# A ring of two buffers in place of three for the split blocks of w_in in the prompt phase

## What is computed

```python
h = rms_norm(x, norm1)
p = h @ w_in                      # 1024 -> 3080 columns: u, v of the gMLP; q, k, v, z; beta, a
y_a = rms_norm(u * (W_s @ gelu(v) + b_s))                # group A, in blocks of 128 rows
q, k, v = silu(causal_conv(q, k, v))                     # group B: width 4, then the gated delta rule
o, S = gated_delta_chunked(q, k, v, g, beta, S0, chunk)  # state S is carried from tile to tile
x = x + concat(y_a, rms_norm(o) * silu(z)) @ w_o
x = x + (silu(h2 @ w_gate) * (h2 @ w_up)) @ w_down       # h2 = rms_norm(x), d_ff = 2816
```

## Time and profile before

| | us |
|---|---|
| median of three executions | 3152.46 |
| lowest and highest | 3148.61, 3154.37 |
| the profiled execution | 3150.51 |
| its span in the trace | 3148.8 |

### The profile page before, as it was taken

How to read it: one execution, slowest core, us unless ns; L and a number is a source line. 1 busy time by engine, 2 the same in 40 slices (tenths; PEclk the granted TensorE clock), 3 DMA queues, 4 the chain that set the end, 5 groups by cost and what they waited for, 6 DMA issues and landing times.

```text
span 3148.8 us, 42004 instructions
## 1 busy us (share of the span) xinstructions
PE 2943.8 (93%) x17132; PEld 2690.0 (85%) x17132; DVE 1418.4 (45%) x2017; ACT 984.2 (31%) x1620; POOL 164.5 (5%) x156
## 2 busy tenths in 40 slices
PE   7689998999998987789999999999999999999998
PEld 6478787878887876689999999999999999999998
DVE  3355556555555543435333343553333335434344
ACT  3233544444444434323212211332112124222212
POOL 2000111111111111200000000000000000000000
PEclk9689999999999988899999999999999999999999
DMA  5245333433333333042122221521222215222220
GB/s 204 76 134 171 98 112 105 130 103 108 96 92 90 115 124 60 15 131 80 54 67 62 65 59 53 187 68 53 67 67 67 62 44 174 81 80 74 73 80 34
DMA packets 352683, 284.44 MB, mean 90 GB/s; under 512 B 14141, under 2 KB 322434, under 8 KB 350514
## 3 DMA queue, kind: packets, MB, share of 16 engines
q1 hardware_dynamic: 352562, 282.78, 29.6%
HBM read 236.97 MB, written 45.78 MB: 90 GB/s over the span
## 4 chain that ended last, share of the span: by engine, by line
PE 54%; DVE 1%; ACT 1%; issue 1%; DVEq 0%; POOL 0%; ACTq 0%; POOLq 0%
PE gate_ps L2828 7%; PE gate_ps L2829 6%; PE gate_ps L2830 6%; PE up_ps L2828 6%; PE up_ps L2829 6%; PE up_ps L2830 6%; PE down_ps L2828 5%; PE down_ps L2829 5%; PE down_ps L2830 5%; DVE w_in_sb L2767 0%; ACT h_hi L2661 0%; DVE w_in_sb L2761 0%; DVE w_in_sb L2822 0%; ACT w_hi L2607 0%; ACT h_hi L2626 0%
## 5 line engine op out<-in xcount | busy, mean ns | idle before, releaser
L2134 PE MATMUL pr_p<-hT_hi_p,w_hi_p 128*128 128x512 f32 x800 | 344.0, 430 | 24.0 <-ACT w_in_sb L1670 21.3
L2828 PE MATMUL gate_ps<-h_hi,w_hi 128*128 128x384 f32 (+1 forms) x1056 | 345.6, 327 | 3.6 <-DVE h_lo L2773 3.4
L2830 PE MATMUL gate_ps<-h_hi,w_lo 128*128 128x384 f32 (+1 forms) x1056 | 345.3, 327 | 0.0
L2829 PE MATMUL gate_ps<-h_lo,w_hi 128*128 128x384 f32 (+1 forms) x1056 | 345.1, 327 | 0.0
L2828 PE MATMUL up_ps<-h_hi,w_hi 128*128 128x384 f32 (+1 forms) x1056 | 344.2, 326 | 0.0
L2829 PE MATMUL up_ps<-h_lo,w_hi 128*128 128x384 f32 (+1 forms) x1056 | 343.9, 326 | 0.0
L2830 PE MATMUL up_ps<-h_hi,w_lo 128*128 128x384 f32 (+1 forms) x1056 | 343.9, 326 | 0.0
L2711 DVE TENSOR_TENSOR w_in_sb<-up_ps,w_in_sb 128x384 f32<-128x384 f32 (+1 forms) x132 | 70.7, 536 | 597.8 <-PE up_ps L2830 597.8
L2136 PE MATMUL pr_p<-hT_hi_p,w_lo_p 128*128 128x512 f32 x800 | 318.6, 398 | 0.0
L2135 PE MATMUL pr_p<-hT_lo_p,w_hi_p 128*128 128x512 f32 x800 | 317.3, 397 | 0.0
L2723 DVE TENSOR_TENSOR w_in_sb<-down_ps,w_in_sb 128x1024 f32<-128x1024 f32 x187 | 228.7, 1223 | 182.8 <-PE down_ps L2830 182.8
(11 more groups left out here) (375 smaller groups left out, 5200.9 us busy)
## 6 DMA issues: line engine op xcount, KB each, us to landing
w_in_sb<-in_w_in SPq DMA_DIRECT2D x100, 512.0 KB, 4.3
w_in_sb<-in_w_gate SPq DMA_DIRECT2D x66, 512.0 KB, 4.0
w_in_sb<-in_w_up SPq DMA_DIRECT2D x66, 512.0 KB, 5.2
w_in_sb<-in_w_down SPq DMA_DIRECT2D x33, 1024.0 KB, 4.9
stream_tiles<-w_in_sb SPq DMA_DIRECT2D x96, 256.0 KB, 2.5
w_in_sb<-stream_tiles SPq DMA_DIRECT2D x16, 1280.0 KB, 6.9
w_in_sb<-in_x_prompt SPq DMA_DIRECT2D x32, 512.0 KB, 5.3
w_in_sb<-in_w_o SPq DMA_DIRECT2D x24, 512.0 KB, 6.7
```

What stands on the lines that cost most here:

```text
L2134: pe.matmul(out, w_h, x_h, start=start, stop=False)
L2828: pe.matmul(out, w_h, x_h, start=start, stop=False)
L2829: pe.matmul(out, w_h, x_l, start=False, stop=False)
L2830: return pe.matmul(out, w_l, x_h, start=False, stop=stop)
```

## The change

`RING_W` goes from 3 to 2, so `w_hi` and `w_lo` have room for two blocks each, and quarter (n, 1) of ACT and of DVE splits block n + 1 in place of n + 2. The split of block 1, which stood in the opening between the norms of the first tiles, goes away there, since quarter (0, 1) makes it. ACT's wait in `split_weights`, on `item_done` at n - RING_W + 1, comes to the same count in every quarter: n for the block n + 2 of before and for the block n + 1 of now. SP's and TensorE's programs are not edited. The matmuls, splits and transfers are the same in number and size.

```diff
@@ -1311,7 +1311,7 @@
 MACRO = 4
 EARLY = 20
-RING_W = 3
+RING_W = 2
@@ -1675,7 +1675,7 @@   (scalar engine)
                 if part == 1:
-                    split_weights(n + 2)
+                    split_weights(n + 1)
@@ -1847,8 +1847,6 @@   (scalar engine, opening)
             for m in range(MACRO):
                 front(m)
-                if m == 1:
-                    split_weights(1)
@@ -2112,8 +2110,6 @@   (vector engine, opening)
                 if m == 0:
                     split_weights(0)
-                if m == 2:
-                    split_weights(1)
```

## The result

| | us |
|---|---|
| before, median of 16 executions | 3150.33 (3146.81 to 3154.37) |
| after, median of 16 executions | 3160.96 (3155.05 to 3167.76, without one of 13719.42) |
| ratio | 1.0032, 95% interval 1.0023 to 1.0040 |
| the profiled execution of after, and its span | 3155.49, 3153.8 |

A forecast was written before the change was run, and what follows sets the result against it. TensorE was taken as the bound, busy for all 144.40 us while only items run. Terms 5.1 + 0.2 + 0.2 = 5.5 us (tiles 0, 4, 8) on the median 3152.46 gave 3158.0, range 3152.3 to 3163.

The forecast's parts named there:

- Macro 0 unchanged: Items before tile 0: splits one item later still have 2.4 to 3.7 us to spare, so no time is lost.
- SP's queue as the place of the cost: SP's load of block 27, 52 or 77 waits for a later split, delaying the streams behind it; tile 0's leave about 315.5.
- Tile 0, 5.1 us: At tile 0 TensorE waits 6.3 us for late streams, then half rate 5.4 us; the gMLP product comes 5.1 us late.
- The 2.17 us of the earlier trace used up: At item 26, ACT's delay uses up TensorE's 2.17 us wait for ACT; the late split of block 26 adds nothing.
- Tiles 4 and 8, 0.2 us each: TensorE's 1.8 us wait for streams is covered; ACT's SiLU delay of 0.2 us remains at each tile.
- their flight of 7.2 us: Streams of tiles 4 and 8 leave at 592.0 and land at 599.2 (tile 4's times); 7.2 us also taken at tile 0.
- the upper end, 8.0: Stream flight of 8.0 us, with one more 256 KB store falling into it: 0.8 us more at each tile, +7.9 in all.
- The rival on splits and clock: Items 26, 51 and 76: late splits bind at TensorE and the clock falls too; +8.8 us, 3161.3; chance 0.22.
- Everything behind it keeps that distance: Item 27 starts about 5 us late and everything behind keeps that, with 0.2 us more behind tiles 4 and 8.
- The sign of being wrong: The delay at item 27 is given back before 1154 us, so something other than TensorE carries the tiles.
- The wait on a split: TensorE waits about 1 us for DVE's split of w_in at items 51 and 76, and not in macro 0.
- The chance of "slower": Whole kernel slower by over 0.2% (6.3 us): chance 0.40, against 0.55 for within 0.2% and 0.05 for faster.

The follow-up runs named there:

- the first kernel of the first group: Changed kernel with the streams of tiles 0, 4 and 8 requested ahead of the load of block 27, 52 or 77: 3157.18 against 3151.63, ratio 1.0014.
- neither part late: Changed kernel with streams of tiles 0, 4, 8 requested before the loads and splits of blocks 26, 51, 76 one quarter sooner: 3149.23 against 3151.12, ratio 0.9997.

## Why the prediction was right, and where it was not

**Macro 0 unchanged: right.** 144.48 us from item 0 to 25 in before; in all kernels with the split one item later and the streams of tile 0 in time 143.7 to 144.7. The spare time that was read off by laying each split beside the item that needs it was really there.

**SP's queue as the place of the cost: right.** The streams left at 313.13, on the axis of before 315.5 (2.34 us for the opening), which is the predicted time. With the kernel before and nothing but that delay the step at item 27 appeared, and with the changed kernel and nothing but the request moved it vanished.

**Tile 0, 5.1 us: right in size,** 5.05, 4.99 and 5.03. The steps in between were off and made up for each other. TensorE waited 6.46 us where 6.3 stood, and the half rate lasted 3.9 us behind the wait (to 324.5), not 5.4 (a figure from the earlier trace rows, which end at 398.00; there the low level lasted to 398.6), so item 25 was done sooner; but it is the chain over ACT and DVE that sets the gMLP product, as worked out, and that product came at 338.05, on the axis of before 340.4, where 340.5 stood. TensorE waited 0.85 us for it.

**The 2.17 us of the earlier trace rows used up, no cost of the late split of block 26 on top: right.** Item 26 starts at 329.65 with no wait, and the changed kernel lost no more than the one with its splits in time.

**Tiles 4 and 8, 0.2 us each: the term that was mis-sized.** Tile 4 cost 3.04, 1.66 and 1.06 us, tile 8 0.02, 0.33 and 0.25. The mechanism was the predicted one: TensorE's wait is covered and ACT's delay is left. The streams left at 592.0 us on the axis of before, as predicted. The term that failed is their flight of 7.2 us: it was 8.8, 8.6 and 8.0, so they landed at 600.9, 600.6 and 600.0 in place of 599.2, and ACT's SiLU was 1.89, 1.66 and 1.06 us late in place of 0.2. That is the whole cost in two of the three profiles; in the first the wait of 3.30 us also brought 0.50 of the clock until 607.8, 1.15 us more. I had taken the 7.2 of the earlier trace rows because the neighbours in the queue were the same, and one of them was not: the store of an item had left ahead of the streams and now leaves into their flight. I had that store in the sum, but only as the upper end, 8.0, and that too was under two of the three flights. At tile 8 TensorE waited 1.12 to 1.74 us, covered as predicted, and ACT's delay was 0.01 to 0.32.

**The rival on splits and clock: its sign was right, its mechanism was not.** It asked for a low clock behind the starts of items 51 and 76, from a divided wait. In after these are at 611.9 and 893.0 us, and the granted clock was 1.00 from 612 to 617 and from 893 to 898. Its 3161.3 us stands closer to 3160.96 than my forecast does, and that is luck, since its price was built on a clock that did not fall there. In the changed kernel the late splits add nothing that can be seen to the late streams. A low clock behind item 51 did appear once where the streams were in time: in the first kernel of the first group the clock was at 0.50 from 609.9 to 613.3, behind item 51, and that stretch is 0.86 us longer. What the median has beyond the profiles (8.5 us on average over three comparisons, 6.7 to 7.1 in the profiles' prompt phase) goes with the executions at lower mean clock: those of after at 0.964 to 0.966 took 3155 to 3160 us, those at 0.961 and 0.962 3163 to 3168.

**"Everything behind it keeps that distance": not quite.** Of the 5.0 us at item 27, 0.8 to 1.7 came back by item 46, where the clock was low for a shorter time than in before, and 0.2 to 1.6 were lost again in 52 to 71. The sign of being wrong (given back before 1154 us) did not appear: 6.7 to 7.1 us are left at item 99. The wait on a split stood at item 76 in all three profiles and at item 51 in two, 1.65 to 1.96 us long where about 1 was named.

**The sum and the chances.** 5.5 was forecast, 8.5 measured: 5.0 for tile 0, 1.1 to 3.0 for tile 4 in place of 0.2, about 0.2 for tile 8, what the clock gave and took between the tiles, and some 1.5 to 2 that no one profile shows. The profiled executions of after are themselves only 5.0, 1.1 and 5.0 us longer than that of before, since item 0 starts 2.2 to 6.4 us sooner in them; the prompt phase and the medians carry the account, not the spans. Part of the hit is luck: forecast and range were built on 3152.46, a median of three, and before came out at 3150.33; the same range on that would have ended at 3160.9, just under the 3160.96 measured. The forecast stood 0.8 us under the bound of 0.2%, and at tile 4 there was no cover left for a flight over 7.2 us, so every longer one had to add. The chance of "slower" ought to have been larger than that of "the same" for this reason.

## What to carry to other kernels

A buffer less in a ring cost nothing here where the step that fills it still ended before its reader, and this can be read off the profile by pairing each step with its reader. It cost time where the step that frees another buffer came later, a queue waited for that, and something urgent stood behind the wait: list what each queue has behind every wait that the change delays, and move the urgent request ahead of it. And where a transfer becomes the step that all wait for, a single row is not its duration: its flight here was 6.7 to 8.8 us with nearly the same neighbours, and at tiles 4 and 8 what it landed after ACT's SiLU was due was lost one for one. So look at every engine that waits for the transfer, and at what covers each: here it was ACT that counted, though TensorE's wait was the longer one.

## What the runs showed of the hardware

- A load of 512 KB issued 0.54 us ahead went with a flight of 1280 KB on the same queue of 6.9 to 7.5 us at tile 0, against 6.0 without it, and of 7.2 to 8.8 us at tile 4, against 6.5. That the load is the cause is not shown: with no load ahead the same transfer took 5.7 to 7.4 us at tile 12.
- One and the same wait of TensorE, 1.62 us at the same place of the program, left the granted clock at 1.00 in one profile and at 0.63 in two others, a difference of 3.0 us for the item behind it. A wait of 6.46 us was followed by 3.9 us at the 1.2 GHz level (granted clock 0.50), one of 3.30 us by 5.9, and one of 3.29 us at the same place in another profile by none.
- The spread goes with it. On one chip the eleven executions with neither part late reached from 3148.59 to 3154.77 us (nine of them within 2.3 us), the kernel before from 3147.86 to 3154.81, and those with the splits late by 0.7 us from 3147.55 to 3161.66.
